# Low passes of the feed-forward weights run ahead, one order for all product groups, first value weight in another place

## What is computed

```
def swiglu(h, w_gu, w_down):
    gu = h @ w_gu
    g, u = jnp.split(gu, 2, axis=-1)
    return (jax.nn.silu(g) * u) @ w_down

for l in range(2):
    if l == 0:
        x = x + gmlp_mixer(rms_norm_2(x, a_norm[0]), ...)
    else:
        k, v = shared_kv(x, kv_norm, kv_w)
        x = x + diff_attention(rms_norm_2(x, b_norm[0]), k, v, b_w_q[0], ...)
    x = x + swiglu(rms_norm_2(x, ffn_norm[l]), ffn_w_gu[l], ffn_w_down[l])
return rms_norm_2(x, final_norm)
```

## Time and profile before

| what | value |
|---|---|
| median of 3 runs | 2065.85 us (2062.56 to 2073.36) |
| the profiled execution, its own time | 2069.45 us |
| its span | 2067.6 us |
| TensorE busy | 1943.3 us, 94% |
| VectorE busy | 1326.9 us, 64% |
| ScalarE busy | 1024.7 us, 50% |
| granted TensorE clock, mean | 0.98 |
| first feed-forward, from its first matmul | 1015.5 to 1401 us |
| attention | 1410 to 1654 us |
| second feed-forward | 1672 to 2056 us |

### The profile page before, as it was taken

One profiled execution on the slowest core, in us unless ns is written; L12 is line 12 of the kernel. 1 busy time (PEld: TensorE's weight loads), 2 busy tenths in 40 slices (PEclk: granted clock), 3 DMA queues, 4 the chain that ended last, 5 costly groups with the idle time before them and its releaser, 6 DMA issues.

```text
span 2067.6 us, 23076 instructions
## 1 busy us (share of the span) xinstructions
PE 1943.3 (94%) x8818; PEld 1554.1 (75%) x8818; DVE 1326.9 (64%) x1698; ACT 1024.7 (50%) x1562; POOL 201.9 (10%) x273
## 2 busy tenths in 40 slices
PE   5999999999999999999999989898999978999987
PEld 4768678887888888588877768777677766877876
DVE  6776799999999999635328347273635334714636
ACT  4443288888888888442323224234655232412413
POOL 3201211132111100200100000001111010000001
PEclk9999999999999999999999999999999999999999
DMA  8564599999999999621321421213210223032221
GB/s 297 181 221 147 173 346 367 379 376 364 379 371 368 363 373 338 216 79 62 123 81 42 160 84 39 104 53 114 82 62 21 82 104 110 27 137 82 72 71 41
DMA packets 200027, 366.51 MB, mean 177 GB/s; under 512 B 13514, under 2 KB 84055, under 8 KB 199914
## 3 DMA queue, kind: packets, MB, share of 16 engines
q1 hardware_dynamic: 181152, 343.20, 47.0%
q10 hardware_dynamic: 8714, 11.17, 1.6%
q0 software_dynamic: 10048, 10.62, 1.5%
HBM read 365.05 MB, written 24.65 MB: 188 GB/s over the span
## 4 chain that ended last, share of the span: by engine, by line
PE 84%; DVE 10%; issue 2%; ACT 1%; DMA 1%; POOL 1%; ACTq 0%; DVEq 0%; POOLq 0%
PE ps L349 81%; DVE wlo L295 3%; PE ps L2307 1%; DVE XN L2949 1%; PE ps L2334 1%; DVE raw L218 1%; DMA VR<-in_b_subln 1%; DVE X L2926 1%; PE ps L3121 0%; ACT whi L275 0%; ACT XN L831 0%; DVE acc L346 0%; POOL small L850 0%; PE ps L882 0%; DVE AT5l L2917 0%
## 5 line engine op out<-in xcount | busy, mean ns | idle before, releaser
L275 ACT ACTIVATE whi<-raw 128x1024 fp32r<-128x1024 f32 (+1 forms) x598 | 594.1, 1045 | 377.2 <-PE ps L349 197.9
L295 DVE TENSOR_TENSOR wlo<-raw,whi 128x1024 fp32r<-128x1024 f32 (+1 forms) x598 | 695.5, 1210 | 128.9 <-ACT whi L275 125.0
L2949 DVE TENSOR_TENSOR XN<-XN,ps 128x512 f32<-128x512 f32 x44 | 30.1, 687 | 301.3 <-PE ps L349 301.3
L349 PE MATMUL ps<-hT5h,whi 128*128 128x512 f32 x352 | 142.0, 403 | 26.0 <-DVE wlo L295 25.4
L349 PE MATMUL ps<-hT3h,whi 128*128 128x512 f32 x352 | 141.9, 403 | 23.8 <-DVE wlo L295 23.2
L349 PE MATMUL ps<-hT5l,whi 128*128 128x512 f32 x352 | 141.2, 401 | 0.0
L349 PE MATMUL ps<-hT3l,whi 128*128 128x512 f32 x352 | 141.2, 401 | 0.0
L349 PE MATMUL ps<-hT5h,wlo 128*128 128x512 f32 x352 | 141.1, 401 | 0.0
L349 PE MATMUL ps<-hT3h,wlo 128*128 128x512 f32 x352 | 141.1, 401 | 0.0
L2876 ACT ACTIVATE XN<-ps 128x512 f32<-128x512 f32 x44 | 26.3, 597 | 163.7 <-PE ps L349 161.9
L349 PE MATMUL ps<-whi,XT1h 128*128 128x512 f32 x256 | 102.7, 401 | 1.5 <-DVE XT1l L2390 1.5
(11 more groups left out here) (491 smaller groups left out, 4148.0 us busy)
## 6 DMA issues: line engine op xcount, KB each, us to landing
raw<-in_w_expert_gate SPq DMA_DIRECT2D x64, 1024.0 KB, 7.3
raw<-in_w_expert_up SPq DMA_DIRECT2D x64, 1024.0 KB, 8.2
raw<-in_w_expert_down SPq DMA_DIRECT2D x64, 1024.0 KB, 7.1
raw<-in_ffn_w_gu SPq DMA_DIRECT2D x44, 1024.0 KB, 5.3
raw<-in_ffn_w_down SPq DMA_DIRECT2D x16, 1024.0 KB, 8.6
raw<-in_ada_w SPq DMA_DIRECT2D x24, 512.0 KB, 4.6
raw<-in_a_w_in SPq DMA_DIRECT2D x8, 1024.0 KB, 10.3
raw<-in_kv_w SPq DMA_DIRECT2D x8, 1024.0 KB, 5.9
```

Of the source, the lines that this page charges most:

```text
L275: e.activation(hi[:, c], x, ACT.Copy).then_inc(self.S("w_hi"), 1)
L295: e.tensor_tensor(lo[:, c], halves[h], hi[:, c].bitcast(F32), ALU.subtract).then_inc(self.S("w_lo"), 1)
L349: return e.matmul(o, l, r, start=start, stop=stop, skip_group_check=True)
L2949: e.tensor_tensor(FA[:, f + k, :], FA[:, f + k, :], R.bank(f"fu{l}.{ng}", k)[:, :], ALU.mult).then_inc(*R.free(f"fu{l}.{ng}", k))
```

## The change

The table `ORDER` becomes one order for all groups, (1, 5, 6, 3, 7, 2, 4), and all that handled the other one goes: in the third group, too, product 7 comes before product 2. At its end the square passes and the additions follow the new order (`rows_act`, the end of `ffn_vec`).

In `ffn_vec`, DVE's low passes at the top of a unit go as far ahead as the places allow, like ACT's high passes.

In the plan, place 3 may take the first weight of a feed-forward and only then is left to raw 4 and 5; the first value weight lies in place 3, which is also `SPARE` (`wide` follows by itself), and is loaded to raw 0; its high pass waits until product 2's down weight has had its low pass, since raw 5 lies there (`since`). The second value weight is split while the row blocks are finished, and the first weight is multiplied with all four row blocks before the second (`v_first`); the value products of row blocks 2 and 3 use banks 1 and 4.

```diff
@@ high @@
+            if self.n_hi in self.since:
+                e.wait_ge(*self.since[self.n_hi])
@@ ffn_items @@
-            held = W.place_last[3]
-            W.places = [0, 1, 2]
+            W.places = [0, 1, 2, 3]
...
                 for name, i in pairs:
                     W.split(name, i, 8, 256)
+                    if W.places[-1] == 3:
+                        held = W.place_last[3]
+                        W.places = [0, 1, 2]
...
-            W.places = [0, 1, 2, 3]
-            W.place_last[3] = W.index[f"fd{l}"][-7 + ORDER[-1].index(2)]
@@ plan of attention @@
+        SPARE = 3
+        W.places, W.place_last[3] = [0, 1, 2, 3], -1
+        W.raw_places = [0, 1]
         v_items(0)
+        W.since[W.index["vv"][0]] = (S("w_lo"), 2 * W.index["fd0"][-7 + ORDER.index(2)] + 2)
+        W.places, W.raw_places = [0, 1, 2], [0, 1, 2, 3]
         qk_items(0)
-        SPARE = W.place_of[W.index["vv"][0]][0]
-        W.places = [z for z in range(4) if z != SPARE]
@@ v_plan @@
-                R.plan(f"vv{half}.{tb}", 1, A_, on=rest)
+                R.plan(f"vv{half}.{tb}", 1, A_, on=rest if half == 1 or tb < 2 else keys)
@@ ffn_vec @@
                 for f in range(0, fn, 2):
-                    j = W.index[f"fu{l}"][ng]
-                    W.low(e, j + 1)
-                    if f == fn - 2:
-                        W.low(e, js[0] + 1)
+                    j = W.index[f"fg{l}"][ng]
+                    W.low(e, j + W.depth(j))
+                    if f < fn - 2:
+                        W.low(e, j + 1 + W.depth(j + 1))
...
                 else:
-                    add(f0, order[4], 0)
-                    add(f0, order[4], 1)
+                    add(f0, 7, 0)
+                    add(f0, 7, 1)
                     W.low(e, js[6] + 2)
-                    add(f0, order[5], 0)
+                    add(f0, 2, 0)
+                    add(f0, 2, 1)
                     then(0)
-                    add(f0, order[5], 1)
+                    add(f0, 4, 0)
+                    add(f0, 4, 1)
                     then(1)
-                    add(f0, order[6], 0)
                     then(2)
-                    add(f0, order[6], 1)
                     then(3)
@@ attn_pe @@
+            def v_first():
+
+                for q, j in enumerate(W.index["vv"][0:2]):
+                    w = W.parts(j)
+                    for tb in range(TB):
+                        b = R.claim(e, f"vv0.{tb}") if q == 0 else R.bank(f"vv0.{tb}")
+                        for k in range(4):
+                            kc = 4 * q + k
+                            if tb == 0:
+                                if k % 2 == 0:
+                                    e.wait_ge(*W.half(j, k // 2))
+                                feature(e, 3, kc)
+                            i = mm3(e, b[:, :], [x[:, kc, tb * P:(tb + 1) * P] for x in hT4], [x[:, k, :] for x in w], kc == 0, kc == KC - 1)
+                        if q == 1:
+                            i.then_inc(*R.fill(f"vv0.{tb}"))
...
-            for tb in range(TB):
-                v_rows(0, tb)
+            v_first()
@@ attn_act @@
-            rows_act(e, 0)
+            rows_act(e, 0, lambda i: take("vv", 1) if i == 3 else None)
@@ attn_vec @@
             features_vec(e, 3, hT4, None)
+            take("vv", 1)
```

More of the change, by code:

```diff
@@ L123, in __init__ @@
         self.raw, self.hi, self.lo = [], [], []
-        self.done_by, self.after, self.quads, self.held, self.sum = [], [], [], {}, []
+        self.done_by, self.after, self.since, self.quads, self.held, self.sum = [], [], {}, [], {}, []
         self.mids = 0
@@ L574, in ffn_items @@
                     W.split(name, i, 8, 256)
+                    if W.places[-1] == 3:
+                        held = W.place_last[3]
+                        W.places = [0, 1, 2]
                 first, over, right, low = quad
[L576 removed]
+                W.quad(f"fd{l}", (first, over, low, right), a, ORDER)
                 if f0 == 0:
                     W.held[right] = W.held[low] = held
[L579 to L580 removed]
         ffn_items(0)
@@ L732, in ffn_plan @@
             ng = nd = 0
-            for (f0, fn), order in zip(FG, ORDER):
+            for f0, fn in FG:
                 for f in range(0, fn, 2):
@@ L740, in ffn_plan @@
                 z, v, y = ([R.turn.popleft(), R.turn.popleft()] for _ in range(3))
-                for p in order:
+                for p in ORDER:
                     name = f"fd{l}.{f0}.{p}"
@@ L2973, in ffn_vec @@
                     for tb in range(2):
-                        add(f0, order[m - 3], tb)
+                        add(f0, ORDER[m - 3], tb)
                     W.low(e, js[m] + 1)
@@ L2979, in ffn_vec @@
                         for tb in range(2):
-                            add(f0, order[m], tb)
+                            add(f0, ORDER[m], tb)
                         if m < 6:
```

47 lines of the change are left out of this document (22 added, 25 removed).

## The result

| what | before | after |
|---|---|---|
| median of 4 runs each, us | 2067.97 (2062.56 to 2073.36) | 1978.89 (1975.06 to 1982.80) |
| the profiled execution | 2069.45 | 1977.55 |
| its span | 2067.6 | 1975.7 |
| granted clock, mean | 0.98 | 0.996 |

The ratio is 0.957, with a 95% interval of 0.954 to 0.960: faster by 89 us, somewhere between 82 and 96. The forecast was 1976.0, with a range of 1966 to 1996.

The account below looks back on a forecast made before the run. TensorE was taken to bound the kernel, with pauses from VectorE's order. Terms 74+3.2+12.8+1.9 = 91.9 took 2069.45 to 1977.5, or 1974 from the median; the forecast was 1976 us, range 1966 to 1996.

Parts of the forecast that it names:

- What bounds the kernel: TensorE, busy 94% of the span; 80 us at stake in the two feed-forwards by start to start.
- Low passes ahead: Feed-forwards: all 15 waits on `wlo` go, with half clock and restarts behind them; 74 us gained.
- Third group in the common order: Feed-forwards' third group: product 7 before product 2 costs nothing, at most 0.5 us twice.
- First value weight in place 3: Start of the values: TensorE's 3.24 us wait at the last product goes; 3.2 us gained, bounds 0 and 4.5.
- Place of the next stage's weights: Output projection to second feed-forward: transition falls from 17.8 to 4.9 us; 12.8 us gained, bounds 10 and 13.
- The end: Kernel's tail: the last row block's scaling starts about 1.9 us earlier, bounds 0 and 3.
- The sum: All terms: 74+3.2+12.8+1.9 = 91.9 us less than the profiled 2069.45.
- The clock did not stay low: Rival in the feed-forwards: something other than pauses lowers the clock, 22 us stay, 1998; chance 0.07.
- The second transition did not keep its length: Rival before the second feed-forward: ScalarE or a load holds the up weight, 12.8 us back, 1989; chance 0.06.
- TensorE met no new wait on loads or high passes: Rival in the feed-forwards: run-ahead meets a new wait, pauses of 2.20 us stay, 2030; chance 0.04.
- TensorE's 345 us without a rest did not lower the clock: Slower rival in the feed-forwards: clock falls because TensorE never rests, 2098 at clock 0.85; chance 0.02.
- Half rate at the start of the second feed-forward: Rival: too little TensorE work in the 5 us before it, 2.4 us lost, 1978.4; chance 0.15.

Follow-up runs that it names:

- the run without the second step: Changed kernel with only the next gate weight's low pass ahead of the multiply, not the next up weight's: 1980.33 us, ratio 0.955.
- The other banks for the values: Changed kernel with value products of row blocks 0 and 1 in banks 1 and 4, those of 2 and 3 in banks 2 and 3: 1977.68 us.
- two further runs: Changed kernel with the second feed-forward's first up weight kept in place 2: 1992.44 us; kernel before with that weight split later: 2056.98 us.
- the kernel with the gate pass ahead: Kernel before, with the gate weight's low pass moved ahead of the two sums before a group's last unit: 2042.98 us, ratio 0.986.
- the kernel with both edits: Changed kernel with swapped value banks and row block 1 scaled between the additions of blocks 2 and 3: 1978.40 us, ratio 0.956.

## Why the prediction was right, and where not

**What bounds the kernel.** Right. The stake was read as 80 us from start to start, not 53 from busy time. The two feed-forwards, first to last matmul, lost 385.31 + 383.66 - 2 x 344.7 = 79.5. Of this, 48.7 and 3.3 were waits; 27.5 was half clock and restarts, forecast 22.2 and 3.8, with 1.9 more around 1395. The pieces of the chain before show the first of these: 2.8 to 2.9 us behind each of the four pauses of 5.07 and 1.6 behind each of six more, 21 us.

**Low passes ahead, 74.** 73.3 by the kernel with this part alone. The mechanism is shown from both sides, by this part alone and by all but this part. It was costed with both weights running ahead; the run without the second step shows that the gate weight alone carries it.

**Third group in the common order, 0.** No new wait: the two waits of 0.5 us on `X` are those that the kernel before had as well (1.0 us of the stake was left for them). No run has this part alone.

**First value weight in place 3, 3.2.** From the first feed-forward's start to the values 356.81 us, against 359.94 in the kernel with the low passes alone: 3.1. It comes about in two steps. Counted from the feed-forward's start, the last product ends 6.2 us earlier than in that kernel (its wait of 3.4 us and the half clock behind it are gone). Then 3.0 us are given back up to the values: TensorE waits 3.4 us among the transposes for the normalisations, where it waited 1.0, and the 3.9 us for the seventh feature stay. The other banks for the values remove most of those 3.9. No run has this part alone either.

**Place of the next stage's weights, 12.8.** 12.9, and two further runs show the cause: the long transition comes back with the place alone, and goes without the change when the pass is not in the way. ScalarE's longest wait for a place there is 2.10 us, where it had stood for 25.15.

**The end, 1.9.** This step failed. The last block's addition did move, from 2.9 us behind the last matmul's start to 0.4 us, but its scaling starts at 5.31 us, where it was 5.29. "Following additions, squares and POOL as before" took POOL's durations from a place where VectorE did not scale beside it. In the new order the scaling of block 1 lies on block 2's root, and the tail stays at 12.1. The trace of the kernel before had the sign of it: POOL's L845 took 1.31 us beside each of the last two long scalings.

```profile
2057.24 1.28 DVE L346 SCALAR_TENSOR_TENSOR X<-X,small,GF 128x1024 f32<-128x1024 f32 x1 [1.71 <-POOL small L850]
...
2057.29 1.31 POOL L845 TENSOR_SCALAR small<-small 128x1 f32<-128x1 f32 x1
```

What the new order gave is inside the last product: from the second feed-forward's start to the end of the span it is 356.81 us against 357.5 with the low passes alone, 0.7. Two stops of TensorE of 0.2 to 0.3 us each for the additions, and the slower matmul behind each, are gone there.

**The sum.** 91.9 forecast, 91.9 between the spans; the equality is luck, since the parts miss by up to 1.2 us and executions of the kernel before lie up to 11 us apart. The end was 1.2 too high and the first term 0.7; 1.0 ahead of the first feed-forward and 0.9 in attention, where the half clock at the values was shorter, had not been counted. By the medians the gain is 89 and 87 us in two measurements, with the spread of the runs in both.

**The rivals.** The clock did not stay low: 1.00 in both windows. The second transition did not keep its length. TensorE met no new wait on loads or high passes. ScalarE's high passes in the first feed-forward follow TensorE (20 waits, 92.4 us) and only once a load (3.9 us). TensorE's 345 us without a rest did not lower the clock. Half rate at the start of the second feed-forward, which had a chance of 0.15, did not come either: the piece of 1389 matmuls takes 315.12 us there and 315.15 in the first. Nor did any other profiled execution start the second feed-forward at half rate, with 5 us or with 18 us of mostly transposes and waiting ahead. The prediction had worked out 2.4 us more for this place by the rule of the Trainium skill (TensorE: Matmul & The Clock Gate, Part 4: PE-mode transpose) that transposes do not count as busy in the same way; the rows here do not bear that out.

## What to carry to other kernels

When an engine works through a list in order, look at what it was idle on before the late instruction: 18 us of idling ahead of a multiply, with the urgent pass behind it, is an order to be changed, and moving just the one pass that is due first is enough. A place or buffer that comes free late costs more than its own wait, since all that stands behind the waiting pass comes late too; read the chain for what is queued, not for who waits. Take durations for a moved step from rows with the same neighbours, on the engines that run beside it too.

## What the runs showed of the hardware

**The same pause, with and without half clock.** In the kernel with everything but the low passes, the pause of 2.20 us ahead of 1063.62 is followed by a half-clock stretch; the same pause in the kernel before shows none.

```profile
1063.62 0.63 PE L351 MATMUL ps<-hT3h,whi 128*128 128x512 f32 x1 [2.20 <-DVE wlo L297]
```

The window from that matmul on:

```profile
1063.50:1067.10 3.60, 3.48 (x9) 2.74 (x10) 3.38 (x3) 0.00 (x0) 0.00 (x0) 0.54 0.34 104
```

Within one execution, too, they differ: of the nine pauses of 2.20 us between units of the kernel before, four were followed by a piece of 93 matmuls that took 1.6 us more than the others. Behind the pauses of 5.07 us the piece of 357 matmuls was longer than the 81.2 us of the kernel with the gate pass ahead in each chain that was read, but not by the same: 2.8 to 2.9 us in the kernel before, 1.4 to 2.8 in that with everything but the low passes. What decides between them no run here shows.

**A half-clock stretch can fall where it costs little.** In the kernel with the other banks it lay over the transposes, and the values began at full clock:

```profile
1368.30:1371.80 3.50, 3.37 (x19) 2.75 (x18) 1.60 (x4) 0.88 (x2) 1.31 (x3) 0.59 0.04 11
1372.80:1376.20 3.40, 3.30 (x14) 2.74 (x15) 3.40 (x7) 3.38 (x6) 0.00 (x0) 1.00 0.02 5
```

In the changed kernel it lies on the first eight value matmuls (0.52, above). In the kernel with both edits neither place shows it: the piece of 272 matmuls takes 62.40 us against 63.82.

**VectorE's scaling stretches POOL.** 0.57 us became 1.63 and 0.22 became 1.31 beside an instruction of 1.28 us with two SBUF inputs. The POOL instruction that had started 0.02 us ahead of such a scaling (1961.71 and 1961.73 in the changed kernel) kept its 0.22. Beside the additions, which read one input from PSUM, POOL's instructions kept their 0.2 and 0.6.
